# The opening of a two-layer diffusion block on one Trainium2 core: packed vector load, filter network first, filter spectra folded by token parity

## What is computed

```python
def adaln(cond, w, b):                       # 9 groups of 1024 per layer: shift, scale, gate, three times
    m = silu(cond) @ w + b

def half_ffn(x, shift, scale, gate, w_in, w_out, g, b):
    h = x * (1 + scale) + shift
    a, u = split(h @ w_in, 2)
    return layernorm(ALPHA * x + 0.5 * gate * ((silu(a) * u) @ w_out), g, b)

def hyena_filters(L, w1, b1, w2, b2, w3, sin_freq):      # L = 512 and 256; needs no token data
    feats = concat([t, cos(ang), -sin(ang)])             # L x 33
    h = sin(sin_freq[0] * (feats @ w1 + b1))             # L x 64
    h = sin(sin_freq[1] * (h @ w2 + b2))
    h = (h @ w3).reshape(L, 2, 512) * window[:, None, :]
    return h[:, 0], h[:, 1]                              # h_fwd, h_bwd

def bidir_fftconv(u, h_fwd, h_bwd, bias):
    k = concat([h_fwd, zeros(1), reversed(h_bwd[1:])])
    K = rfft(k, n=2 * L)                                 # the filter spectra
    ...
# reference: per layer adaln, half_ffn, mixer (layer 0: Hyena and RG-LRU, layer 1: latent attention), half_ffn
```

## Time and profile before

| | us |
|---|---|
| median of 3 runs (2917.24 to 2925.12) | 2918.26 |
| the profiled execution | 2922.01 |
| its span, first to last instruction | 2920.0 |
| of it up to the first product of unit A (L3031) | 106.43 |
| up to A's latent half | 115.60 |
| up to unit B | 126.6 |

### The profile page before, as it was taken

One profiled execution on the slowest core, in us unless ns is written; L12 is line 12 of the kernel. 1 busy time (PEld: TensorE's weight loads), 2 busy tenths in 40 slices (PEclk: granted clock), 3 DMA queues, 4 the chain that ended last, 5 costly groups with the idle time before them and its releaser, 6 DMA issues.

```text
span 2920.0 us, 46373 instructions
## 1 busy us (share of the span) xinstructions
PE 2843.5 (97%) x17295; PEld 2463.3 (84%) x17295; DVE 2006.7 (69%) x3255; ACT 1042.5 (36%) x1655; POOL 286.7 (10%) x395
## 2 busy tenths in 40 slices
PE   6999999999999999999999999999999999999998
PEld 3688999988875888998998889999978998878887
DVE  3567767776767477676776887777776887554545
ACT  1422323325660342232223432333265665422123
POOL 1000000001000100101000000000004654000000
PEclk8999999999999999999999999999999999999999
DMA  7434432221213233534431122222310101233331
GB/s 256 163 130 152 133 133 72 65 78 42 61 53 123 87 101 117 172 128 152 135 101 59 44 65 70 74 70 67 96 41 21 29 21 44 68 111 96 101 99 46
DMA packets 301704, 268.20 MB, mean 92 GB/s; under 512 B 31175, under 2 KB 257327, under 8 KB 301456
## 3 DMA queue, kind: packets, MB, share of 16 engines
q1 hardware_dynamic: 278960, 187.38, 21.4%
q0 software_dynamic: 21760, 76.03, 7.5%
q10 hardware_dynamic: 864, 3.15, 0.3%
HBM read 261.28 MB, written 5.24 MB: 91 GB/s over the span
## 4 chain that ended last, share of the span: by engine, by line
PE 89%; DVE 5%; DMA 2%; ACT 2%; issue 1%; POOL 0%; SPq 0%; DVEq 0%; ACTq 0%; POOLq 0%
PE PSALL L2959 15%; PE PSALL L2960 14%; PE PSALL L2961 14%; PE PSALL L3276 8%; PE PSALL L3277 8%; PE PSALL L3278 8%; PE PSALL L2870 2%; PE PSALL L3031 2%; PE PSALL L3032 2%; PE PSALL L3033 2%; PE PSALL L3704 1%; PE PSALL L3689 1%; PE PSALL L2912 1%; PE PSALL L2984 1%; PE PSALL L3569 1%
## 5 line engine op out<-in xcount | busy, mean ns | idle before, releaser
L2084 DVE SCALAR_TENSOR_TENSOR X<-PSALL,GATE,X 128x512 f32<-128x512 f32 x480 | 279.9, 613 | 102.2 <-PE PSALL L2961 101.5
L3276 PE MATMUL PSALL<-HHI,WSH 128*128 128x384 f32 x816 | 273.4, 335 | 5.8 <-DVE HLO L2282 5.8
L3277 PE MATMUL PSALL<-HLO,WSH 128*128 128x384 f32 x816 | 273.5, 335 | 0.0
L3278 PE MATMUL PSALL<-HHI,WSL 128*128 128x384 f32 x816 | 272.7, 334 | 0.0
L2959 PE MATMUL PSALL<-GHIA,WHIW 128*128 128x512 f32 (+1 forms) x618 | 218.2, 353 | 15.3 <-DVE X L2084 12.4
L2960 PE MATMUL PSALL<-GLOA,WHIW 128*128 128x512 f32 (+1 forms) x618 | 214.0, 346 | 0.0
L2961 PE MATMUL PSALL<-GHIA,WLOW 128*128 128x512 f32 (+1 forms) x618 | 213.5, 346 | 0.0
L2959 PE MATMUL PSALL<-GHIB,WHIW 128*128 128x512 f32 (+1 forms) x618 | 213.2, 345 | 0.0
L2961 PE MATMUL PSALL<-GHIB,WLOW 128*128 128x512 f32 (+1 forms) x618 | 213.2, 345 | 0.0
L2960 PE MATMUL PSALL<-GLOB,WHIW 128*128 128x512 f32 (+1 forms) x618 | 213.2, 345 | 0.0
L1199 ACT ACTIVATE WSH<-RAW 128x512 fp32r<-128x512 f32 x204 | 129.0, 632 | 224.7 <-DVE RAW L2161 153.0
(11 more groups left out here) (421 smaller groups left out, 7120.7 us busy)
## 6 DMA issues: line engine op xcount, KB each, us to landing
RAW<-in_ffn_w_in_dram SPq DMA_DIRECT2D x176, 512.0 KB, 4.1
ADA<-in_ada_w_dram POOLq DMA_DIRECT2D x144, 512.0 KB, 5.6
RAW<-in_ffn_w_out_dram SPq DMA_DIRECT2D x88, 512.0 KB, 3.8
RAW<-in_ev_w_in_dram SPq DMA_DIRECT2D x20, 512.0 KB, 4.3
WRAW<-in_mla_w_q_up_dram SPq DMA_DIRECT2D x16, 288.0 KB, 3.1
RAW<-in_ev_w_out_dram SPq DMA_DIRECT2D x8, 512.0 KB, 4.4
RAW<-in_mla_w_in_dram SPq DMA_DIRECT2D x8, 512.0 KB, 4.2
RAW<-in_mla_w_out_dram SPq DMA_DIRECT2D x8, 512.0 KB, 4.3
```

The costliest lines, as they stand in the source:

```text
L2084: dve.scalar_tensor_tensor(X[:, m, lo:lo + n], down_bank(m, s, 2), GATE[:, j, m, s:s + 1], X[:, m, lo:lo + n], ALU.mult, ALU.add).then_inc ...
L3276: te.matmul(out, w_hi, hi[block](k), start=(k == 0), stop=False)
L3277: te.matmul(out, w_hi, low[block](k), start=False, stop=False)
L3278: x = te.matmul(out, w_lo, hi[block](k), start=False, stop=(k == 3))
```

## The change

All of it lies in the first part.

- The host packs all vectors into one array: one load instead of one for each piece, and FVEC (four columns) in one load too. FEATS, FW1, FVEC and VIN are issued first, then FW2 and FW3, then x, ctx and the window WINT. Transposes of x wait for groups of three loads (`xin_in`); the last group is both ctx blocks and WINT.
- TensorE starts with filter layer 0, then the vectors; group 0's first half, the transposes of x token block by token block, and filter layer 1 are interleaved.
- Tokens are ordered even before odd, frequencies in pairs f and L-1-f. For such a pair the even tokens' part E and the odd tokens' part O give E+O and E-O (cosine; for the sine O-E). `spectra(r)` makes E and O for one pair of frequency blocks; three calls make 20 products instead of 40. ScalarE copies E (`even_take`), VectorE makes the sum and the difference (`combine`).
- w3's sum and difference are formed once (WSUM), so that four of the six token blocks need two window products on VectorE and no sums. The blocks that hold token 0 keep the old form.
- SPL moves on VectorE from before the coefficients to `ffn0`, behind the gate.

The diff, cut to its core:

```diff
-        for name, first, t, r, n in vec_pieces():
-            sp.dma_start(VIN[r:r + n, t, :], rows[name][first:first + n, :]).then_inc(vin_in, 16)
+        for dst, src in ((FEATS, A["feats"]), (FW1, A["hy_filt_w1"][0]), (FVEC, A["filt_vec"])):
             sp.dma_start(dst[:, :], src).then_inc(flt_in, 16)
+        sp.dma_start(VIN[:, :, :], A["vecs"]).then_inc(flt_in, 16)
...
+    XIN_PART = (0, 1, 1, 1, 2, 2)
...
+        for b in range(LB // 2):
+            sp.dma_start(FWDL[:, b, :, :, :], A["flt_l"][b]).then_inc(tab_in, 16)
+        sp.dma_start(FWDC[:, 0, :, :, :], A["flt_c"][0]).then_inc(tab_in, 16)
...
+        def even_take(r, v):
+            act.wait_ge(f_pe, 2 + 2 * TB + 2 * r + v + 1)
+            if r:
+                act.wait_ge(f_spec, 4 * (r - 1) + 2 * v + 2)
+            act.activation(KE[:, v, :], PS[4 + 2 * v][:, :], ACT.Copy).then_inc(f_even, 1)
+
+        def spectra_out(r):
+            act.wait_ge(f_spec, 4 * (r + 1))
+            for n in range(2):
+                act.dma_start(KF[2 * r + n], KOUT[:, r % 2, n, :, :]).then_inc(kf_out[r % 2], 16)
...
+        def combine(r, v):
+            dve.wait_ge(f_even, 2 * r + v + 1)
+            if r == 2:
+                dve.wait_ge(kf_out[0], 32)
+            odd = PS[5 + 2 * v][:, :]
+            dve.tensor_tensor(KOUT[:, r % 2, 0, v, :], odd, KE[:, v, :], ALU.add).then_inc(f_spec, 1)
+            a, b = (KE[:, v, :], odd) if v == 0 else (odd, KE[:, v, :])
+            dve.tensor_tensor(KOUT[:, r % 2, 1, v, :], a, b, ALU.subtract).then_inc(f_spec, 1)
...
+        def spectra(r, between=None):
+            T, blocks, t0 = (FWDL[:, r - 1], LB, 0) if r else (FWDC[:, 0], CB_, LB)
...
+                for odd in range(2):
+                    for t in range(blocks // 2):
+                        b = odd * blocks // 2 + t
+                        x = te.matmul(PS[4 + 2 * v + odd][:, :], T[:, b, v, :], FILT[t0 + b][:, v, :],
+                                      start=(t == 0), stop=(t == blocks // 2 - 1))
...
+        te.wait_ge(flt_in, 16 * 4)
         filter_layer(0)
+        vectors()
+        te.wait_ge(cond_ok, 2)
+        ada_products(0, first)
+        x_turn(0)
         filter_layer(1)
+        for t in range(1, 4):
+            x_turn(t)
+        ada_products(0, second)
+        x_turn(4)
+        te.wait_ge(f_sin, 2)
+        te.wait_ge(f_dve, 11)
+        filter_rows(0)
+        x_turn(5)
+        filter_rows(1)
+        te.wait_ge(tr_taken, plan["ada_first"].tr)
         ada_columns(0, 2)
         ada_products(1, first)
+        for t in range(2, TB):
+            filter_rows(t)
+        te.wait_ge(tab_in, 16 * 3)
         spectra(0)
+        spectra(1, lambda: ada_products(1, second))
         ada_columns(1, 2)
+        spectra(2)
         ada_products(2, first)
```

More of the change, by code:

```diff
@@ L129, with packed @@
 VT = -(-VROWS // P)
[L132 to L143, removed]
+def packed(inputs):
+    rows = np.concatenate([np.asarray(inputs[name]).reshape(-1, P) for name in VEC])
+    rows = np.concatenate([rows, np.zeros((VT * P - VROWS, P), rows.dtype)])
+    columns = [inputs["hy_filt_b1"][0], inputs["hy_filt_b2"][0], inputs["hy_sin_freq"][0, 0], inputs["hy_sin_freq"][0, 1]]
+    return {"vecs": rows.reshape(VT, P, P).transpose(1, 0, 2), "filt_vec": np.stack([np.asarray(v) for v in columns], 1)}
 def build(nc, A, out):
@@ L338, in build @@
     PS = [PSALL[:, b, :] for b in range(8)]
-    vin_in, xin_in = sem("vin_in"), sem("xin_in")
+    xin_in = [sem(f"xin_in{n}") for n in range(3)]
+    XIN_PART = (0, 1, 1, 1, 2, 2)
     const_ok = sem("const_ok")
@@ new lines, in _ @@
+        sp.dma_start(VIN[:, :, :], A["vecs"]).then_inc(flt_in, 16)
+        for dst, src in ((FW2, A["hy_filt_w2"][0]), (FW3, A["hy_filt_w3"][0])):
+            sp.dma_start(dst[:, :], src).then_inc(xin_in[0], 16)
+        for t in range(TB):
+            src = A["x"][0, t * P:(t + 1) * P, :] if t < LB else A["ctx"][0, (t - LB) * P:(t - LB + 1) * P, :]
+            sp.dma_start(XIN[:, t, :], src).then_inc(xin_in[XIN_PART[t]], 16)
+        sp.dma_start(WINT[:, :, :], A["win"]).then_inc(xin_in[2], 16)
@@ L1916, in _ @@
         assert nco[0] == COEF_FIRST - 1
-        for a in range(2):
-            for m in range(KC):
-                low("h0", a, m)
+        for m in range(3):
+            low("h0", 0, m)
+        combine(2, 0)
+        for m in range(3, 6):
+            low("h0", 0, m)
+        combine(2, 1)
+        for m in range(6, KC):
+            low("h0", 0, m)
+        for m in range(KC):
+            low("h0", 1, m)
         next_unit("ffn0", "B")
@@ L2914, in spectra, with x_turn @@
                 x.then_inc(f_pe, 1)
+                if v == 0 and between is not None:
+                    between()
         first, second = range(ADA_RING), range(ADA_RING, KC)
-        te.wait_ge(flt_in, 16 * 8)
+        def x_turn(t):
+            te.wait_ge(xin_in[XIN_PART[t]], 16 * 3)
+            for half in range(2):
+                e = 2 * t + half
+                te.wait_ge(tr_taken, VT + max(e - 2, 0))
+                for m in range(4):
+                    x = te.transpose(PS[e % 3][:, m * P:(m + 1) * P], XIN[:, t, (4 * half + m) * P:(4 * half + m + 1) * P], ID[:, :])
+                x.then_inc(tr_done, 1)
@@ L3789 @@
     arrays, args = {}, {}
-    tables = constants()
+    tables = {**constants(), **packed(inputs)}
     for name in _INS + tuple(tables):
```

276 lines of the change are left out of this document (114 added, 162 removed).

## The result

The changed kernel takes **2899.48 us** (median of 4 runs, 2897.27 to 2902.23) against 2918.66 us for the kernel before beside it (4 runs, 2917.24 to 2925.12). The ratio is 0.9936, 95% interval 0.9920 to 0.9952: 0.64% faster, with both ends beyond the 0.3% that can be told from no change. The forecast was 2895.7, the range 2882 to 2907. The profiled execution took 2900.35 us with a span of 2898.6, against 2922.01 and 2920.0: 21.7 less, 21.4 of them in the span.

What follows compares the result with a forecast made beforehand. TensorE, busy 97% of the span, was taken to bound the kernel; 9.7 us from the start and 12.9 from the fold make 22.6, so 2922.0 becomes 2899.4, on the median's scale 2895.7 us, range 2882 to 2907.

Steps and rivals of the forecast that it cites:

- blocks 2 to 5: Filter row blocks behind the second stall: 14.2 us at the lower clock, plus 1.4 of VectorE for the last block.
- M: Start of unit A's latent half on TensorE, same list behind it in both programs: 93.0 instead of 115.60, 22.6 us earlier.
- the loads of group 0: Start: 9.5 MB including ada_w, x, ctx and window, at 400 GB/s, there at about 28 us.
- The rival of late loads: Start: at 330 GB/s loads arrive at 33 instead of 28, SPL's cover shrinks; 2901 to 2905 us, chance 0.17.
- the spectra's start: TensorE's spectra, behind the filter blocks, start at 60.2 us instead of 69.88, 9.7 earlier.
- 9.7 from the start and 12.9 from the fold: Split of the 22.6 us gain; the 12.9 is of 17.2 from the fold and from what stood beside it.
- The early clock: Rival: filter rows without a pause bring full clock to filter blocks and call 0; 10.7 us more, 2885, chance 0.18.
- M's last step: Unit A's context half: eighth chunk's remainder at 88.7, second column block 2.8 us until 91.9, then group 2's loads.
- The clock staying down through unit A, 2928: Rival: TensorE stays at the lower clock from 60.2 through unit A; 9.8 us slower, chance 0.03.
- Costed at nothing: Combinations under spectra but two, windows' sums under TensorE, SPL moved to `ffn0` with 1.8 us of cover left: no cost.
- the lock-out: Start: GpSimd's four load issues could each wait for a VectorE step in two-port mode; up to 3 us worse.
- The scale: Profiled execution taken as 3.8 us above the median, so 2899.4 profiled becomes 2895.7 as median.

Runs made afterwards that it cites:

- e6: The changed kernel once more with nothing edited: median 2898.76 us over 6 runs, 0.9924 to 0.9955 of the kernel before.
- e1: The changed kernel with the spectra's products done twice, so TensorE has its 40 products again: 2918.13 us, level with the kernel before (ratio 0.9997).
- e2: The changed kernel with the vectors loaded in 16 pieces ahead of the filter inputs, as before: 2900.70 us.
- e8: The changed kernel with idle identity products in TensorE's waits before group 0's last blocks and before group 1's fourth block: 2898.62 us.
- e12: e8 with only the stores of spectra calls 1 and 2 held until group 2's last ada_w block has landed: 2898.55 us.
- e10: The changed kernel with unit B's first loads and the stores of calls 1 and 2 held until group 2's last ada_w block landed: 2907.28 us.

## Why the prediction was right

The time was right, by a sum whose two parts do not add as it said.

| step | predicted | after | 
|---|---|---|
| filter layer 0 | 7.1 | 5.76 |
| group 0's first half ends | 16.2 | 15.8 |
| filter layer 1 | 19.1 | 19.0 |
| group 0's last product ends | 29.0 | 32.85 |
| blocks 0 and 1 end | 38.8 | 44.06 |
| second stall with its products | 5.7 | 5.3 |
| blocks 2 to 5, until the spectra start | 15.7 | 9.5 |
| spectra start | 60.2 | 58.87 |
| columns | 74.8 | 73.7 |
| first h, eighth chunk's remainder | 77.5, 88.7 | 76.36, 87.75 |
| M | 93.0 | 94.65 |
| the profiled execution | 2899.4 | 2900.35 |

**Mis-sized: the loads of group 0.** 9.5 MB at 400 GB/s gave 28 us. The eighth block landed at 31.7, when the engines had moved 344 GB/s times 31.7 us, 10.9 MB: tables and weights issued behind the named loads share the engines with them. Another 1.2 us went into the two times eight transposes ahead of blocks 0 and 1, 1.90 us each at half clock instead of 1.3. The rival of late loads had this mechanism, at 33; 3.7 of its 5 us came.

**Right by luck: the spectra's start.** The 5.3 us lost there came back in blocks 2 to 5, which ran at full clock in this one execution, where the forecast had half. Behind block 4 came VectorE's work on the last two blocks, 4.0 us against the 1.4 of the forecast (the rival had 4.2); TensorE waited 2.47 of them. In e6 it was the other way about: blocks 0 and 1 at full clock (2.19 and 1.91), blocks 2 to 5 at half (13.42), spectra at 59.17.

**Wrong: 9.7 from the start and 12.9 from the fold.** e1 takes away the fold's saving and keeps the early start, and is left with none of the time; e2 starts filter layer 0 at 14.46 again and loses none. So the two parts are not shares that can be added. What the fold would be worth with the spectra starting at 70 no run shows. The sum treated the spectra's start as a point from which M follows. It does in before, where TensorE alone binds the spectra. After, it is one of three chains that end within some us of each other: TensorE's, ScalarE's through stores and h, and the transfers. That the three meet I had written for ScalarE and the loads of group 2; what I left out is that the loads do not hang on the spectra's start alone but on the 8.9 MB that are moved in the same stretch, because the stores and the weights now fall into it with both halves of group 2 (in before 62 to 97 us carried 6.0 MB, and group 2's second half came behind).

**The early clock: right mechanism, wrong price.** That rival gave 2885, with spectra at 50.8 (60.2 less 3.5 and 5.9). e8 gave it its condition, blocks 0 to 5 at full clock, and the run was 2898.6. The loads of group 0 and the fill had the spectra start at 56.69, call 0 took 6.59 us, near the lower clock's 6.9, and the rest ended in the waits for ada_w and the half clock behind them. Only with the transfers held does M move further (88.94 in e12).

**M's last step.** From the eighth chunk to the end of unit A's second column block it took 4.99 us (87.79 to 92.78) where the sum had 3.2 (88.7 to 91.9). TensorE had waited 2.13 us for h; it was still at full clock over 86 to 88 and had 0.63 over 88 to 92. That the wait is what lowered it is argued, not shown by an edit. Then the products of group 2's second half stand behind it with 1.86, of which the sum had counted 0.6. ScalarE's chain up to the eighth chunk was 1 us shorter than predicted. Net, 1.65.

**The clock staying down through unit A, 2928.** It did not: the granted clock was 1.00 from 64 to 88 us in after, also in every variant's second and third call. (The reading behind it had a slip that changes nothing: 7.26 us is what one group of eight spectra instructions would take at the lower level, not two.)

**Costed at nothing, rightly.** SPL ended at 114.25 and unit A's next remainder at 119.16 (predicted 114.3 and 119.2), TensorE's first use of it at 122.96 without a wait. The four issues of GpSimd beside VectorE's work took 0.53 us each; one of them, and what VectorE ran beside it:

```profile
13.01 0.53 POOL L833 DMA_DIRECT2D ADA<-in_ada_w_dram  x1 [8.43 <-PE PSALL L2882]
```

```profile
12.27 2.92 DVE L1722 SCALAR_TENSOR_TENSOR FZ<-FN,FZ 64x768 f32<-64x768 f32 x3
```

So the lock-out of the Trainium skill's page SBUF — State Buffer, which would have cost up to 3 us, does not show in these four. Three stood beside this operation and the fourth beside a sum of two tensors (16.14, L1726); no row shows which mode they ran in, so the rule itself is not tested. The row of 0.53 that the prediction held against it stood beside a sum of windowed rows (L1784), not beside a window product.

**The scale.** The profiled executions differ by 21.7; the medians by 19.2. I had put the changed kernel's profile as far above its median as before's, 3.8; it was 0.9 above. These 2.9 us and the sum's own miss of 1.0 (2899.4 against 2900.35) make the 3.8 us between 2895.7 and 2899.48.

## What to carry to other kernels

Work that is taken off the bounding engine is worth its time only as far as the next chain; list the chains that end at the same mark, and add up the bytes that are to move in the shortened stretch, those that nobody waits for there too. A stretch that gets shorter draws the transfers around it together: ask which of them can wait, and who waits for each, down to a wait for stores in another engine's list. And before a gain is shared out between two parts of a change, undo each: here undoing the fold cost the whole gain and undoing the packed load cost nothing, though the profile shows both as time saved.

## What the runs showed of the hardware

- The same instructions in the same order ran at either clock in two executions of one kernel: blocks 2 to 5 took 7.06 and 13.42 us. Idle products in TensorE's waiting ahead of them gave 7.1 four times out of four.
- Filter rows ran for 12 to 14 us without a pause, most of them at half clock (0.50 over 49.3 to 54.7 in e6); in every profile the spectra behind them were at full clock by the second half of their second call (3.63 us for eight instructions, in e1 7.07 for sixteen).
- A block of 512 KB took 15.6 us from issue to landing at 344 GB/s of traffic from both queues, 6.5 with stores and unit B's weights held back, and 3.9 when the engines had just stood still (after, issued at 44.77; 0 GB/s over 40.4 to 44.1).
- In three places a wait of TensorE was followed by a lower clock: behind 5.38 us it came back at 0.50 (e10, 108 to 112 us), behind 1.29 and 1.67 us it ran at 0.50 (e8, 84 to 88), and behind 2.13 us it was at 1.00 over 86 to 88 and at 0.63 over 88 to 92 (after).
